# Slicing the attention queries by partition instead of loading them into a zero-filled tile, and keeping a scan mask as a constant

## The reference, cut to what matters

```python
def probs(qc, kc):                      # qc, kc: one half (32 wide) of each of 8 heads
    s = jnp.einsum('bqhd,bkhd->bhqk', qc, kc).astype(jnp.float32) * scale + bias
    return jax.nn.softmax(jnp.where(mask, s, NEG), axis=-1)

a = probs(q[..., :32], k[..., :32]) - lam * probs(q[..., 32:], k[..., 32:])
o = jnp.einsum('bhqk,bkhd->bqhd', a, v)

# HGRN2: cumulative sum of log f inside a chunk of the sequence
b = jnp.cumsum(logf, axis=1)

# PEER: 8 heads x 16 experts per token, rows of two tables of 16384 x 1024
act = gelu(einsum('td,thkd->thk', xb, u_tab[eidx]))
y   = einsum('thk,thkd->td', g * act, v_tab[eidx])
```

## Time and profile before

| | us |
|---|---|
| median of 3 runs | 4148.15 |
| lowest and highest | 4138.77, 4152.79 |
| profiled execution, its own time | 4148.15 |
| its span, first to last instruction | 4146.4 |
| TensorE busy | 2874.5 (69%) |
| VectorE busy | 2505.5 (60%) |
| GpSimd busy | 2258.2 (54%) |
| ScalarE busy | 1054.7 (25%) |
| share of the 16 DMA engines' time in the gathers' queue q0 | 78.4% |
| mean granted TensorE clock | 0.758 of full speed |

### The profile page before, as it was taken

The page is one execution under the profiler, slowest core; times in us unless marked ns, Lnnn a source line. Parts: engine busy times, 40 slices in busy tenths (PEclk is TensorE's granted clock), DMA queues, the critical chain, the costliest instruction groups (busy, mean ns, idle before and its releaser), DMA issues.

```text
span 4146.4 us, 51705 instructions
## 1 busy us (share of the span) xinstructions
PE 2874.5 (69%) x18028; PEld 1564.4 (38%) x18028; DVE 2505.5 (60%) x6789; ACT 1054.7 (25%) x2882; POOL 2258.2 (54%) x2365
## 2 busy tenths in 40 slices
PE   7889998777487757785777588758784665333365
PEld 6745644444254424442443254325442322000011
DVE  2445756766776687658766876686668556644400
ACT  3412212322232232222332323232322111110121
POOL 1102443665566566556566656565556666666665
PEclk9989999777588768786788688868876576555566
DMA  7635798999999999899999999999999999999998
GB/s 207 191 125 180 265 338 273 377 372 366 345 365 362 363 365 360 323 347 367 340 369 374 370 348 375 351 361 328 350 363 349 376 360 352 364 370 365 364 365 318
DMA packets 544257, 1389.62 MB, mean 335 GB/s; under 512 B 59496, under 2 KB 223776, under 8 KB 544000
## 3 DMA queue, kind: packets, MB, share of 16 engines
q0 software_dynamic: 335024, 1215.35, 78.4%
q1 hardware_dynamic: 196752, 161.33, 12.2%
q10 hardware_dynamic: 12224, 9.63, 0.9%
HBM read 1352.93 MB, written 33.04 MB: 334 GB/s over the span
## 4 chain that ended last, share of the span: by engine, by line
PE 19%; issue 16%; DMA 14%; POOL 10%; another core or an unknown queue 6%; DVE 5%; ACT 3%; SPq 1%; ACTq 0%; DVEq 0%; POOLq 0%
DMA d_vb<-in_peer_v_dram,d_eidT 7%; PE d_pY L1719 5%; POOL d_vb L1689 5%; POOL d_ub L1670 4%; DVE d_ub L1883 2%; DMA d_ub<-in_peer_u_dram,d_eid 2%; PE d_pS L856 2%; PE d_pS L841 2%; PE r_pB L1608 2%; PE r_pB L1435 1%; PE d_pS L909 1%; DMA r_side<-out_v_sample_dram 1%; DMA t_shared<-scratch_kT 1%; DMA d_ub<-in_peer_v_dram,d_eidT 1%
## 5 line engine op out<-in xcount | busy, mean ns | idle before, releaser
L1883 DVE CUSTOM_DVE_ANT_0 d_ub<-d_ub,d_pX 128x1024 f32<-128x1024 f32 x1024 | 1240.3, 1217 | 628.0 <-DMA d_ub<-in_peer_u_dram,d_eid 508.2
L1670 POOL DMA_INDIRECT d_ub<-in_peer_u_dram,d_eid x1152 | 1124.5, 976 | 879.8 <-DVE d_hdot L1883 390.9
L1689 POOL DMA_INDIRECT d_vb<-in_peer_v_dram,d_eidT x1096 | 1050.8, 959 | 867.4 <-PE d_pY L1719 390.7
L1719 PE MATMUL d_pY<-d_vb,d_dg 128*32 128x256 f32 x8768 | 913.8, 506 | 805.6 <-DMA d_vb<-in_peer_v_dram,d_eidT 553.7
L1719 PEld LDWEIGHTS d_pY<-d_vb,d_dg 128*32 128x32 f32 x8768 | 255.2, 127 | 1358.2 <-issue 1195.6
L1758 ACT ACTIVATE d_dg<-c_late_sb,d_wgtT 128x32 f32<-128x32 f32 x1152 | 335.9, 315 | 1343.4 <-PE d_pY L1719 786.4
L703 PE MATMUL d_pX<-d_wq,d_vb 128*128 128x512 f32 (+3 forms) x1536 | 470.3, 459 | 15.6 <-DMA d_vb<-in_w_in_dram 9.0
L703 PEld LDWEIGHTS d_pX<-d_wq,d_vb 128*128 128x128 f32 x1536 | 269.5, 199 | 179.5 <-issue 111.6
L841 PE MATMUL d_pS<-t_shared,t_qz 128*128 128x512 f32 (+3 forms) x384 | 200.6, 654 | 65.5 <-DMA t_shared<-scratch_kT 29.3
L856 PE MATMUL d_pS<-t_mdg,t_E 128*128 128x128 f32 x1152 | 181.2, 311 | 59.2 <-issue 36.1
L856 PEld LDWEIGHTS d_pS<-t_mdg,t_E 128*128 128x128 f32 x1152 | 162.6, 218 | 110.8 <-issue 74.7
(11 more groups left out here) (278 smaller groups left out, 3531.4 us busy)
## 6 DMA issues: line engine op xcount, KB each, us to landing
d_vb<-in_w_in_dram SPq DMA_DIRECT2D x68, 512.0 KB
d_ub<-in_peer_u_dram,d_eid POOLq DMA_INDIRECT x1152
d_vb<-in_peer_v_dram,d_eidT POOLq DMA_INDIRECT x1096
r_side<-in_cache_k_dram SPq DMA_DIRECT2D x16, 1024.0 KB
r_side<-in_cache_v_dram SPq DMA_DIRECT2D x16, 1024.0 KB
d_wo<-in_w_out_dram SPq DMA_DIRECT2D x6, 2048.0 KB, 7.9
d_wo<-in_peer_w_q_dram SPq DMA_DIRECT2D x4, 2048.0 KB, 9.1
scratch_h<-t_shared SPq DMA_DIRECT2D x9, 512.0 KB
```

The costliest lines, as they stand in the source:

```text
L1670: pool.indirect_dma_start(out=ub[:, g % R, :], out_offset=None, in_=io["peer_u"][0], in_offset=off).then_inc(u_in[g % R], 16)
L1689: pool.indirect_dma_start(out=to, out_offset=None, in_=io["peer_v"][0], in_offset=off).then_inc(landed, 16)
L1719: m = nc.tensor.matmul(pY[q * QT:(q + 1) * QT, g % 2, :], dg[:, n % DG, :], rows[:, q * QD:(q + 1) * QD], start=k % QT == 0, stop=k % QT = ...
L1883: nc.vector.tensor_tensor_reduce(out=ub[:, g % R, :], in0=ub[:, g % R, :], in1=xflat if i else xn_of(0), scale=1.0, scalar=0.0, op0=ALU.mu ...
```

## The change

Queries: `qz` and its zeros are gone. The queries of a whole tile (128 x 512) come by one DMA into `shared`, columns 0 to 511, at the tile's start. `scores` takes 32 partitions of them as stationary operand and the same 32 partitions of the keys as moving operand, so it contracts over 32 rows instead of 128. TensorE waits for the queries once a tile, and SyncE no longer waits for `c_ready` before the first load. Mask: a table `carry` (128 x 512) is added to the small constants, the two memsets of each recurrence go, and the scan reads the table.

```diff
+    carry = np.tile((np.arange(W) % SUB != 0).astype(np.float32), (P, 1))
-    small = np.concatenate([np.eye(P, dtype=np.float32), np.ones((P, P), np.float32), pick, block, inchunk,
+    small = np.concatenate([np.eye(P, dtype=np.float32), np.ones((P, P), np.float32), pick, block, inchunk, carry,
...
-        qz = ph.sb("t_qz", [P, 4, P])
...
-        kT, V, osq = part(shared, 512, NPT, P), part(shared, 1536, NPT, P), part(shared, 2560, DH, VD)
+        qT, kT, V, osq = part(shared, 0, 4, P), part(shared, 512, NPT, P), part(shared, 1536, NPT, P), part(shared, 2560, DH, VD)
...
-            step(nc.vector.memset(qz[:], 0.0))
...
             if t:
-                if i == 0:
-                    sp.wait_ge(c_ready, 1)
+                sp.dma_start(qT, sc["qT"][t].rearrange("p (h n) -> p h n", h=4)).then_inc(in_q, 16)
                 for hp in range(4):
...
-                    for g in range(4):
-                        sp.dma_start(qz[32 * g:32 * g + 32, g, :], sc["qT"][t][32 * g:32 * g + 32, hp * P:(hp + 1) * P]).then_inc(in_q, 16)
...
-                    pe.wait_ge(in_q, 64 * (4 * prompts[i] + hp + 1))
...
+                r = 32 * (2 * h2 + m)
                 for a in range(0, nk, 512):
                     n = min(512, nk - a)
-                    ins = nc.tensor.matmul(pSf[:, at_bank[m] + a:at_bank[m] + a + n], qz[:, 2 * h2 + m, :], kTf[:, a:a + n], start=True, stop=True)
+                    ins = nc.tensor.matmul(pSf[:, at_bank[m] + a:at_bank[m] + a + n], qT[r:r + 32, hp, :], kTf[r:r + 32, a:a + n], start=True, stop=True)
...
             if t:
+                pe.wait_ge(in_q, 16 * (prompts[i] + 1))
                 pe_at = []
...
-            step(nc.vector.memset(flat(rl), 1.0))
-            step(nc.vector.memset(rl.rearrange("p h (c i) -> p (h c) i", i=SUB)[:, :, 0:1], 0.0))
...
-            nc.vector.tensor_tensor_scan(flat(rb), flat(rl), flat(re), 0.0, ALU.mult, ALU.add).then_inc(b_done, 1)
+            nc.vector.tensor_tensor_scan(flat(rb), carry, flat(re), 0.0, ALU.mult, ALU.add).then_inc(b_done, 1)
```

More of the change, by code:

```diff
@@ L90 @@
 _at = 0
-for _name, _w in (("ident", P), ("ones", P), ("pick", P + SUB - 1), ("block", P), ("inchunk", NSUB),
+for _name, _w in (("ident", P), ("ones", P), ("pick", P + SUB - 1), ("block", P), ("inchunk", NSUB), ("carry", W),
                   ("rows", 64), ("second", 1), ("places", NCAND)):
@@ L344, in layer @@
         ident, places = small("ident"), small("places")
-        ones, pick, blockm, inchunk, rows_ = (small(n) for n in ("ones", "pick", "block", "inchunk", "rows"))
+        ones, pick, blockm, inchunk, carry, rows_ = (small(n) for n in ("ones", "pick", "block", "inchunk", "carry", "rows"))
         wo_in, wq_in, half_done = [ph.sem(f"d_wo_in{n}") for n in range(2)], ph.sem("d_wq_in"), ph.sem("d_half_done")
```

## The result

The changed kernel takes 4184.25 us, the median of 7 runs (4164.06 to 4188.80), against 4148.15 us for the kernel before (7 runs, 4138.77 to 4160.52). The ratio is 1.0076, with a 95% interval of 1.0052 to 1.0100: slower by 0.5 to 1.0%, where no change was forecast, and above the upper end of the range, 4170 us. The profiled execution took 4155.09 us and was the shortest of the changed kernel; its granted clock is 0.746, that of the timed runs 0.738 to 0.743, and in the profiled execution before it was 0.758. So the profile shows the kinds of the losses, but only part of their size: 7 of the 36 us.

What follows compares the result with a forecast made beforehand. TensorE was taken to bound the first 710 us, DMA gathers the rest. First stretch +2.9 us and second -5 (-2 - 1 - 2) gave -2 together: 4146 us, forecast as no change; 8-in-10 range 4116 to 4170 us.

Steps and rivals of the forecast that it cites:

- rival 3: TensorE in the mixers: granted clock falls by a tenth because 32 of 128 rows work; 4190 us, chance 0.05.
- The sign that I had set for rival 3: Granted clock of the second stretch, 710 to 4100 us: 0.68 instead of about 0.72 would show the clock falling.
- What TensorE's time is worth, a fifth: Second stretch: one fifth of TensorE's time or waits reaches the end; 11 us becomes 2, and 3 becomes 1.
- a gain of 3 us and one of 11: Second stretch: 3 us less TensorE time from overlap against borders, and 11 us fewer waits for keys.
- The borders: TensorE switching between 32-row score calls and 128-row calls: 0.17 us each, 7.8 us in the first stretch, 10.9 in the second.
- rival 2: TensorE, tiles 1 and 2: border costs win, from 0.25 us a border without overlap; 4165 us, chance 0.15.
- The overlap: Narrow score pairs: two halves run beside each other, halving each pair; 3.6 us won in the first stretch, 18 in the second.
- the +4.2 that the forecast had: First stretch, where TensorE is the bound: 7.8 us lost by borders less 3.6 won by overlap.
- Larger constants: Start of the kernel: 262 KB more constants load ahead of all weights, +0.8 us.
- the second step: Query loads: keys issued up to 1.75 us earlier, TensorE waiting 11 us less for them, worth 2 us.
- Rival 4: SyncE late for another reason, keys' path not shorter: the 2 us go, 4148 us; chance 0.54 together with the forecast.
- the 4 us of the forecast: New query loads in the second stretch: 2 us from shorter waits for keys and 2 us from fewer packets.

Runs made afterwards that it cites:

- run 4: Kernel before plus a 16-column matmul over 32 rows ahead of each of the 128 score calls, which stay at 128 rows: 3950.61 us, ratio 1.0078.
- run 1: Kernel before with score calls over 32 rows of `qz`; loads, zeros and mask unchanged: 3971.36 us against 3916.19, ratio 1.0146.
- run 7: Kernel before with score calls over 64 rows, both halves of a head sharing rows: 4193.7 us against 4151.06, ratio 1.0103.
- run 6: Separate small program of TensorE matmuls over 128, 32 and 64 rows, with pauses and without, computing nothing of the reference: 1452.29 us, one execution.
- run 2: Changed kernel with score calls over all 128 rows, halves not separated, so other experts are chosen: 3896.56 us, ratio 0.9956 to the kernel before.
- Run 5: Kernel before plus a 16-column matmul over 128 rows ahead of each score call: 4165.33 us against 4151.06, ratio 1.0045.
- run 8: Kernel before with a second zeroed query tile, so the next pair's queries load behind the keys; 128 rows: 4140.93 us against 4151.06, ratio 0.9987.
- run 9: Kernel before with one query load a tile, widened on VectorE into `qz`; scores over 128 rows, mask memsets kept: 3908.52 us against 3916.51, ratio 0.9973.
- run 11: The changed kernel unaltered, measured once more on the chip of the later runs: 3939.40 us, ratio 1.0058 to the kernel before.
- run 12: Kernel before with score calls over 32 rows and the old loads, measured once more: 3975.54 us, ratio 1.0146.
- run 10: Changed kernel with four query loads at the tile's start, in 512 B packets, instead of one load: ratio 1.0050 to the kernel before.
- run 3: Changed kernel without its mask part, the table gone and the two memsets back: ratio 1.0065 to the kernel before.

## Why the prediction was wrong, step by step

**The clock is the step that failed.** The sum has no term for it: "The clock of the second stretch stays near 0.72". Only rival 3 said that it would fall because 32 of 128 rows work, gave 4190 us, and got a chance of 0.05. The clock fell in the change from 0.758 to 0.740, in the rows alone by 0.025, and the loss goes with it: run 4 has borders and no fewer rows, and neither its clock nor its neighbours moved; runs 1 and 7 have fewer rows, and both did; run 6, without pauses and borders, shows the rows alone setting the level. The sign that I had set for rival 3, 0.68 in the second stretch, was too strict: the profile has 0.70. The argument that sank it, "the clock is 0.96 up to 710 us, where the 64-row group stands too", was a poor witness, since that stretch is dense with matmuls over 128 rows, and even now its clock is 0.96. The danger was in the second stretch, where the clock already moved between its two levels (0.72) and TensorE was busy only 2.77 of 10 us at a wide score call. In size the rival was too harsh on the clock (a tenth; 2 to 3% came) and too mild on what it costs (a fifth). An estimate for run 1: 0.0255 / 0.776 = 3.3% of the 2188 us that TensorE is busy after 710 us in run 2 is 72 us, and the end came 55 us later, borders among them. That 4190 us lies so near the measured 4184 is in part luck: two errors in opposite directions.

**What TensorE's time is worth, a fifth, was low if anything.** Run 5 gives half or so outside the first stretch, run 4 a quarter. This did not sink the forecast: it multiplied a gain of 3 us and one of 11, so a higher worth would have moved the sum towards faster, away from what was measured. Why the time lost with the clock reaches the end more fully than added matmuls do is not shown. The forecast also read a mean DMA share of 0.97 as cover. One hundredth of it is 0.01 x 3390 = 34 us, as large as the whole loss, so a share given to two places can't rule such a loss out.

**The borders were sized right.** 0.17 was taken; 0.17 and 0.20 stand in the timeline, 0.15 by runs 4 and 5. What rival 2 asked for, 0.25 and no overlap, did not come. **The overlap was right**, and complete: 0.86 to 0.63 us with a border in tile 2. Single calls got two borders and no overlap. In the first mixer, the first score call after the change starts 3.4 us later than before (at 152.09 instead of 148.67), and the fourth 4.6 later (161.97 instead of 157.39): three calls at 2 x 0.19. So of the 8.0 us at the first gather of `peer_v`, 3.4 came before any score call, and the other 4.6 fit the +4.2 that the forecast had for borders less overlap. Larger constants were to cost 0.8; but run 1, without them, has its first score call at 151.65, and run 2, with them, at 149.4. So the start itself varies by about as much, and single profiles do not settle it.

**The keys came earlier, as the second step said**, and a wait for them is worth about a fourth (run 8). Rival 4 is out. **But the new loads win more than the 4 us of the forecast**: 0.44% in run 2, 0.27% in run 9, and 36 us (0.9%) where the rows are 32 (runs 11 and 12). Only the last is clear of the 0.13% of run 8; the intervals of runs 2, 8 and 9 overlap or touch. The packets are not it (run 10), nor is the mask (run 3). What is left is the freed time of SyncE's queue and of the two engines that zeroed or waited; no run tried these one by one, and why the loads are worth more at a low clock stays open. Run 2 chooses other experts, so its figure is the weakest of the three.

**The mask** was put at -0.6 us, and nothing was seen.

Put together: rows of 32 cost 1.46% (runs 1 and 12, 55 and 59 us), loads and mask give back 0.88% beside them (runs 12 and 11), and 0.58% are left (run 11); 0.76% were measured where the kernel before takes 4148 us. Of the 55 us some 10 go by borders (206 of them at the price of runs 4 and 5; some 20 us at the upper end of their intervals), less what the overlap won, and the rest with the clock. This division is worked out, not measured, since no run holds the clock while it takes 32 rows.

The Trainium skill's "TensorEngine Tiling (Array Packing)", section "Key Properties", says that a change of the tiling mode drains the engine; the 0.76 us gaps and the 0.15 to 0.20 us of a border agree. The Trainium skill's "TensorE: Matmul & The Clock Gate", "Part 3: Packing small matmuls", says that products on different row groups run side by side; the 2.08 us for eight against 2.07 for four agree.

## What to carry to other kernels

At one clock a matmul over fewer rows takes the same time (2.07 us for four instructions over 32 and over 128 rows, run 6), and yet it costs: at the edge between the two clock levels it can lower the clock for all its neighbours, so padding with zeros to 128 rows may be the cheaper form, as it was here. Before narrowing an operand, look at the granted clock of the stretch where the calls stand, not at a dense one. Where a change holds a gain and a loss, run each alone: here the loads were good for 0.3 to 0.9%, and the rows buried it.

## What the runs showed of the hardware that was not expected

- The granted clock follows the rows in use. Without pauses: 1.00 over 128 rows, 0.50 over 32, TensorE busy 25.00 of 25 us in both (run 6). In the kernel: 0.760 with 128 rows, 0.746 with 64 (run 7); 0.776 with 128, 0.7505 with 32 (run 1).
- Of three calls in a group, one over 32 rows is enough for 0.50 instead of 1.00 (run 6; this section has borders too).
- Matmuls on two row groups overlap completely (2.08 us for eight, 2.07 for four), and a border between 32 and 128 rows costs 0.15 to 0.20 us at full clock and 0.30 at half.
- The same kernel took 3916 us in two groups of runs and 4151 in a third, with clocks of 0.776, 0.771 and 0.760. The third group and one of the others carry the same chip number, so the runs do not show whether the chip makes the difference.
